# Bringing ScalarE's tables in ahead of the first gates and three attentions, in a fused two-model block kernel

## The chip, the cores and the metric

The kernel runs on one core of one Trainium2 chip, as one launch. Its time is the device time of that launch in microseconds. A core has TensorE (PE in the profile), VectorE (DVE), ScalarE (ACT), GpSimd (POOL) and SyncE (SP), each with an instruction stream of its own; they meet by semaphores.

## What is computed

The input is one sequence of 512 tokens with 1024 features in fp32. A first block is followed by a second block of two layers and a last RMS norm. Cut to what matters:

```python
# first block
h = rms_norm(x, norm_gain); proj = h @ w_in          # q_n, kc, vc, ks, vs, kw, vw, gates, z_n, q_d, k_d, v_d, qi, ki, wi, z_d
g = sigmoid(gate_logits)
o_nsa = g0 * compressed + g1 * selected + g2 * window # 8 heads of 64, times silu(z_n)
o_dsa = attention over the 128 best keys by score = sum_h relu(qi_h . ki) * wi_h   # times silu(z_d)
x = x + concat(o_nsa, o_dsa) @ w_out
# second block, for each of 2 layers
cos, sin = rope_tables(positions)
mod = c @ w_ada + b_ada
h = rms_norm(x) * (1 + sc) + sh; proj = h @ w_in
y_a = rg_lru(conv(x_lru))                             # sigmoid gates, exp(log_a), sqrt
c_q, c_kv = rms_norm(q_down), rms_norm(kv_down)       # latents, 256 and 128 wide
y_b = causal softmax attention of 8 heads of 192, from c_q, c_kv and a roped key   # mla
y = sigmoid(gate_a) * y_a + sigmoid(gate_b) * y_b
x = x + g_m * (y @ w_out); x = x + g_f * (silu(gate) * up) @ w_ffn_out
```

## The kernel before, in words

Everything is written by hand: one function per engine (`block.sync`, `block.gpsimd`, `block.scalar`, `block.vector`, `block.tensor`) writes out that engine's stream in order, with waits on semaphores. There is no scheduler; an engine does its instructions strictly in the order written. X is held transposed, 8 tiles of 128 features by 512 tokens.

**Weights.** All weights come as one stream of 512 KB slots into a ring of seven buffers (RAW). ScalarE copies a slot to its rounded high part (WH, `split_through`, L601), GpSimd (or VectorE for some) subtracts to get the low part (WL, L512), and TensorE does each product as three matmuls (L1894, L1895, L1896: high by high, low by high, high by low). A buffer is refilled once its slot has been passed.

**PSUM.** TensorE takes its eight banks in turn (`claim`) and waits there for whoever read the bank's last content.

**ScalarE's order.** In the first block ScalarE evicts the projection groups in the order 0, 1, 4, 2, 3, 5, 6 (`evict_group`). Group 0 has the index queries (MISC, L704), the index weights (L705) and the gate logits; L707 takes the sigmoid of these, the first in the program. L744 follows with a logarithm for the recurrence's parameters, for which VectorE waits (L1309) before it ropes the index queries. Between groups ScalarE takes the relus of the index scores (`relus(1)`, `relus(2)`, `relus(3)`), which VectorE sums to scores (`index_scores`, L1404, L1409) and reduces by rounds of the eight largest (`topk_round`). Group 2 is the query projection. The cosine and sine of the second block's positions (cs2, tile `cs`) are one activation, L789, that stands behind all evictions of the first block and ahead of its attention; VectorE has the angles ready by L1363 and reads the result only in the second block (`rope2_tables`).

**The three attentions.** The first block's has 96 units of one head pair and one tile of 128 queries; each layer of the second block has one with 32 units. In unit u TensorE makes the scores, VectorE the negated maximum (nmax, L1508 or L1739), ScalarE the exponential (L825 or L959), and TensorE transposes unit u-3 (L2190 or L2320) and, after an eviction, multiplies by the values. In the second block VectorE also scales the exponentials (L1746, L1748) before they are transposed.

**Before a layer's attention.** After the last gate eviction (`"gb"`, tile SG, L609) TensorE transposes the latents and the roped key, 16 transposes (L1992 on KVR). ScalarE evicts them as the high parts CQH and CKH (L920) and as KPE (L924, L925), VectorE makes the low parts (CQL, CKL, L1720), and TensorE's first query product (L1894 on CQH) waits for the two CQL. The value and query products, their evictions and VectorE's roping follow, and then the attention.

**Tables.** A function that the active table lacks needs an ACT_TABLE_LOAD, which is put in directly before the activation; where the activation has more than one wait, the load stands behind all but the last of them. Copy, Identity, Square and Relu have none ahead of them in this program, but for the very first activation (L657).

Of the kernel before, what the change touches and what calls it, by code (L numbers as in the profile page):

```python
# [34 lines left out]
ACT = mybir.ActivationFunctionType  # L35
F32 = mybir.dt.float32
# [5 lines left out]
P = 128  # L42
# [169 lines left out]
def head_square(g, tt):  # L212

    return NT * list(HEAD_GROUPS).index(g) + tt
# [20 lines left out]
def program(nc, a, known):  # L235

    note = {}
    with ExitStack() as ctx:
# [3 lines left out]
        def at(name, shape, dt, off):  # L242
            return nc.alloc_sbuf_tensor_at(name, shape, dt, offset=base + int(off))
# [11 lines left out]
        def small(name, shape, dt, size=4):  # L255
            off = cur[0]
            cur[0] += (int(np.prod(shape[1:])) * size + 31) // 32 * 32
            return at(name, shape, dt, off)
# [5 lines left out]
        vec1 = small("vec1", [P, 3 * KD], F32)  # L264
# [5 lines left out]
        cs2 = small("cs2", [P, 2, NT, HALF], F32)  # L270
# [11 lines left out]
        W0 = (cur[0] + 63) // 64 * 64 + 128  # L282

        def w(name, shape, dt, kb):

            return at(name, shape, dt, W0 + kb * KB)
# [82 lines left out]
        SHA = w("SHA", [P, S], F32, 64)  # L369
        SPREAD = w("SPREAD", [P, S], F32, 66)  # L370

        bank = [ctx.enter_context(nc.psum_tensor(f"bank{i}", [P, S], F32)) for i in range(8)]
        landed = [ctx.enter_context(nc.semaphore(f"slot_landed{i}")) for i in range(RAW_RING)]
        sem = {name: ctx.enter_context(nc.semaphore(name)) for name in SEMAPHORES}
        step = sem["step"]
        count = dict.fromkeys(SEMAPHORES, 0)

        def mark(name, *key, by=1):

            count[name] += by  # L380
            note[(name,) + key] = count[name]
            return by

        def value(*key):

            if known and key not in known:
                raise KeyError(key)
            return known.get(key, 1)
# [6 lines left out]
        def ring(key):  # L395
            return SLOT[key] % RAW_RING

        def loads(key):

            return 16 * (SLOT[key] // RAW_RING + 1)  # L400

        def last_use(key):

            name, v = known.get(("used",) + key, ("full", 1))
            return sem[name], v

        def raw(key):
            return RAW[SLOT[key] % RAW_RING]

        def hi(key):  # L410
            return WH[WSLOT[key] % SPLIT_RING]
# [4 lines left out]
        def bank_of(*key):  # L416

            return bank[known.get(("bank",) + key, 0)]
# [12 lines left out]
        def first_square(k):  # L431

            return (RELU[:, 0, :], RELU[:, 1, :], TMP[:, 0, :], TMP[:, 1, :])[k % 4]
# [156 lines left out]
        def _(act):  # L590
            split_next = [0]

            def split_through(key, ahead=SPLIT_RING - 1):

                last = min(WSLOT[key] + ahead, len(WEIGHTS) - 1)
                while split_next[0] <= last:
                    k = WEIGHTS[split_next[0]]
                    act.wait_ge(landed[ring(k)], loads(k))
                    if split_next[0] >= SPLIT_RING:
                        act.wait_ge(*last_use(WEIGHTS[split_next[0] - SPLIT_RING]))  # L600
                    nc.scalar.activation(hi(k)[:], raw(k)[:], ACT.Copy).then_inc(sem["w_hi"], mark("w_hi", *k))  # L601
                    split_next[0] += 1

            def evict(dst, *key, func=ACT.Copy, **kw):

                act.wait_ge(sem["full"], value("full", *key))
                b = bank_of(*key)
                n = int(np.prod(dst.shape[1:]))
                return nc.scalar.activation(dst, b[0:dst.shape[0], 0:n], func, **kw).then_inc(  # L609
                    sem["read_act"], mark("read_act", *key))  # L610

            def square(tag, k, sq):
                if tag == "n1":
                    if k >= 4:
                        act.wait_ge(sem["n1_added"], value("n1_added", tag, max(1, k - 4)))
                    dst = first_square(k)
                else:
                    if k >= 2:
                        act.wait_ge(sem["sq_added"], value("sq_added", tag, max(1, k - 2)))
                    dst = sq[:, k % 2, :]  # L620
                nc.scalar.activation(dst, X[:, k, :], ACT.Square, scale=float(D) ** -0.5).then_inc(
                    sem["square"], mark("square", tag, k))
# [59 lines left out]
            for k in range(KD):  # L682
# [7 lines left out]
            nc.scalar.activation(lt[:, 1], lt[:, 0], ACT.Exp, scale=-1.0).then_inc(  # L690
                sem["lru_par"], mark("lru_par", 1))
            split_through(("p1", 1, 3), 0)

            def evict_group(g):

                split_through(("p1", g, 3), 0 if g in (2, 3, 6) else SPLIT_RING - 1)
                if g == 0:
                    act.wait_ge(step, value("rstd", "n1"))
                for tt in range(NT):
                    act.wait_ge(sem["full"], value("full", "p1", g, tt))  # L700
                    b = bank_of("p1", g, tt)
                    rstd = stat[:, 1, tt:tt + 1]
                    if g == 0:
                        nc.scalar.activation(MISC[:, tt, :], b[:, 0:384], ACT.Identity, scale=rstd)  # L704
                        nc.scalar.activation(gate[:, tt, 24:28], b[:, 408:412], ACT.Identity,  # L705
                                             scale=stat[:, 2, tt:tt + 1])
                        nc.scalar.activation(gate[:, tt, 0:24], b[:, 384:408], ACT.Sigmoid, scale=rstd).then_inc(  # L707
                            sem["read_act"], mark("read_act", "p1", g, tt))
                    elif g < 5:
                        if g in HEAD_GROUPS:  # L710
                            i = head_square(g, tt)
                            if i >= 4:
                                act.wait_ge(sem["head_sq_read"], value("head_sq_read", i - 4))
                            n = HEAD_GROUPS[g]
                            nc.scalar.activation(HSQ[:, i % 4, 0:n], b[:, 0:n], ACT.Square, scale=rstd).then_inc(
                                sem["head_sq"], mark("head_sq", i))
                        evict(G[g][:, tt, :], "p1", g, tt, func=ACT.Identity, scale=rstd)
                    else:
                        act.wait_ge(sem["iscore"], value("iscore", 3, 3))
                        evict(Z[:, tt, (g - 5) * 512:(g - 4) * 512], "p1", g, tt, func=ACT.Silu, scale=rstd)  # L720

            def relus(qt):
                n = (qt + 1) * P
                for h in range(1, 4):
                    if qt > 1:
                        act.wait_ge(sem["iscore"], value("iscore", qt - 1, h))
                    evict(RELU[:, h - 1, 0:n], "idx", qt, h, func=ACT.Relu)

            def shift_in(kv):


                act.wait_ge(sem["full"], value("full", "tc", kv))
                b = bank_of("tc", kv)
                act.wait_ge(sem["pool_set"], value("pool_set", 1))
                if kv:
                    act.wait_ge(sem["ca"], value("ca", 0, 1))
                for g in range(2):
                    nc.scalar.activation(KC2[0:DH, g, 0:S], b[g * DH:(g + 1) * DH, :], ACT.Copy)
                    last = nc.scalar.activation(KC2[DH:P, g, 0:S - 1], b[g * DH:(g + 1) * DH, 1:S], ACT.Copy)
                last.then_inc(sem["read_act"], mark("read_act", "tc", kv))  # L740
# [8 lines left out]
            relus(1)  # L749
            shift_in(0)  # L750
            evict_group(2)
            relus(2)
            relus(3)
            split_through(("p1", 3, 0))
# [30 lines left out]
                sem["read_act"], mark("read_act", "tkc"))  # L785


            act.wait_ge(step, value("angles"))
            nc.scalar.activation(cs2[:], cs2[:], ACT.Sin).then_inc(sem["cos_sin"], mark("cos_sin"))  # L789


            def scale_ada(i):
# [57 lines left out]
            for layer in range(LAYERS):  # L850
                L = layer

                def vec(col):
                    return par[:, L, col:col + 1]
# [57 lines left out]
                for n in range(KD):  # L912
                    split_through(("gb", L, n))
                    act.wait_ge(sem["ya_gated"], value("ya_gated", L, n))
                    evict(SG[:, n, :], "gb", L, n, func=ACT.Sigmoid)
                for i in range(3):
                    act.wait_ge(sem["full"], value("full", "tc2", L, i))
                    b = bank_of("tc2", L, i)
                    dst = CQH[:, i, :] if i < 2 else CKH[:]
                    nc.scalar.activation(dst, b[:], ACT.Identity, scale=vec(PQG + i)).then_inc(  # L920
                        sem["c_hi"], mark("c_hi", L, i))
# [1589 lines left out]
```

## Time and profile before

| | |
|---|---|
| median of 3 runs | 1813.1 us (1811.85, 1813.1, 1813.21) |
| the profiled execution | 1810.82 us, of which the span from first to last instruction is 1809.0 |
| PE busy | 1744.4 us (96%) |
| DVE busy | 993.7 us (55%) |
| ACT busy | 731.2 us (40%) |
| POOL busy | 693.9 us (38%) |
| mean granted TensorE clock | 0.992 of full |
| ACT_TABLE_LOAD | 27, 1283 ns each |

Times in the trace are microseconds from the first instruction. A row of a timeline is: start, duration, engine, line, operation, output<-inputs, shape, count, and in brackets the idle time of that engine before the row and what ended it. Rows that follow each other and are alike are merged. Activations overlap their neighbours by about 0.1 us. The end of a matmul in the trace is modelled. The granted clock is a share of 2.4 GHz: 1.00 is 2.4 GHz and 0.50 is 1.2 GHz.

### The profile page before, as it was taken

To read this page: it belongs to the slowest core of one execution; us is meant where nothing else is said; L and a number is where in the kernel's file an instruction comes from. 1 tells how busy PE (TensorE), PEld (TensorE's weight loads), DVE (VectorE), ACT (ScalarE), POOL (GpSimd) and SP (SyncE) were. 2 spreads that over 40 slices of the span, in tenths; PEclk is the share of its full clock that TensorE was granted. 3 is DMA by queue.
4 is the path that set the end of the run, shared out by engine and by line. 5 is a ranking of instruction groups with operands and counts; after the bars stand their busy time and mean duration, and the time that the engine had idled before them with its cause. 6 is when DMAs were issued, how large, how long until landed. Compare 5 with 4: busy or idle time off the path is not lost. (4 is left out here: it accounts for less than half of the span.)

```text
span 1809.0 us, 23187 instructions
## 1 busy us (share of the span) xinstructions
PE 1744.4 (96%) x8313; PEld 1415.0 (78%) x8313; DVE 993.7 (55%) x1653; ACT 731.2 (40%) x1258; POOL 693.9 (38%) x305
## 2 busy tenths in 40 slices
PE   7999998989999999999999999999999999999997
PEld 7777777767888766788888888878766888888886
DVE  5999776484679577633333336989665631111112
ACT  6434665523475554322222223456454342222221
POOL 3424111246430333555545557430211644444442
PEclk9999999999999999999999999999999999999998
DMA  7234010063232224355555542322310322232211
GB/s 251 80 104 140 24 36 24 24 209 120 102 105 93 82 82 136 133 198 186 194 188 199 187 140 97 113 82 94 105 36 27 102 93 93 86 112 93 93 59 47
DMA packets 56632, 197.65 MB, mean 109 GB/s; under 512 B 6993, under 2 KB 8017, under 8 KB 56530
## 3 DMA queue, kind: packets, MB, share of 16 engines
q1 hardware_dynamic: 55666, 194.15, 31.5%
q10 hardware_dynamic: 864, 2.11, 0.3%
q8 instruction: 67, 1.10, 0.3%
q14 instruction: 35, 0.29, 0.0%
HBM read 194.14 MB, written 2.10 MB: 108 GB/s over the span
## 5 line engine op out<-in xcount | busy, mean ns | idle before, releaser
L512 POOL TENSOR_TENSOR WL<-RAW,WH 128x1024 fp32r<-128x1024 f32 x234 | 593.7, 2543 | 876.5 <-ACT WH L601 542.1
L1894 PE MATMUL bank<-HH,WH 128*128 128x512 f32 x1120 | 437.3, 390 | 6.8 <-POOLq L517 5.9
L1895 PE MATMUL bank<-HL,WH 128*128 128x512 f32 x1120 | 436.0, 389 | 0.0
L1896 PE MATMUL bank<-HH,WL 128*128 128x512 f32 x1120 | 435.9, 389 | 0.0
L601 ACT ACTIVATE WH<-RAW 128x1024 fp32r<-128x1024 f32 x259 | 270.5, 1051 | 244.6 <-PE bank L1896 220.0
L1894 PEld LDWEIGHTS bank<-HH,WH 128*128 128x128 f32 x1120 | 210.4, 188 | 52.2 <-issue 8.8
L1896 PEld LDWEIGHTS bank<-HH,WL 128*128 128x128 f32 x1120 | 210.4, 188 | 43.9
L1895 PEld LDWEIGHTS bank<-HL,WH 128*128 128x128 f32 x1120 | 210.4, 188 | 43.3
L1814 DVE TENSOR_TENSOR HF<-SILU,bank 128x512 f32<-128x512 f32 x43 | 29.6, 688 | 301.6 <-PE bank L1896 300.6
L1894 PE MATMUL bank<-HDH,WH 128*128 128x512 f32 x352 | 137.1, 389 | 0.0
L1896 PE MATMUL bank<-HDH,WL 128*128 128x512 f32 x352 | 136.9, 389 | 0.0
L1895 PE MATMUL bank<-HDL,WH 128*128 128x512 f32 x352 | 136.9, 389 | 0.0
L1894 PE MATMUL bank<-WH,HH 128*128 128x512 f32 (+2 forms) x288 | 111.9, 389 | 13.7 <-DVE WL L1259 8.4
L1825 DVE SCALAR_TENSOR_TENSOR X<-bank,mod,X 128x512 f32<-128x512 f32 x32 | 24.0, 751 | 174.0 <-PE bank L1896 174.0
L1896 PE MATMUL bank<-WH,HL 128*128 128x512 f32 (+2 forms) x288 | 110.3, 383 | 0.0
L1895 PE MATMUL bank<-WL,HH 128*128 128x512 f32 (+2 forms) x288 | 110.2, 383 | 0.0
L1042 DVE SCALAR_TENSOR_TENSOR ACC<-RAW,vec,ACC 128x1024 f32<-128x1024 f32 x70 | 106.7, 1524 | 4.0
L1002 ACT ACTIVATE HDH<-HF 128x512 fp32r<-128x512 f32 x44 | 27.8, 632 | 191.2 <-DVE HF L1814 190.4
L526 POOL TENSOR_TENSOR ACC<-ACC,RAW 128x1024 f32<-128x1024 f32 x14 | 33.5, 2393 | 139.4 <-ACT RAW L805 139.1
L609 ACT ACTIVATE SILU<-bank 128x512 f32<-128x512 f32 x43 | 25.7, 597 | 129.9 <-PE bank L1896 129.8
L1508 DVE TENSOR_REDUCE nmax<-bank 128x1 f32<-128x128 f32 (+3 forms) x96 | 46.0, 489 | 57.3 <-PE bank L2183 36.9
L1895 PEld LDWEIGHTS bank<-HDL,WH 128*128 128x128 f32 x352 | 66.1, 188 | 13.7
(370 smaller groups left out, 2903.8 us busy)
## 6 DMA issues: line engine op xcount, KB each, us to landing
RAW<-in_stream SPq DMA_DIRECT2D x363, 512.0 KB, 3.3
out_t<-YA SPq DMA_DIRECT2D x8, 256.0 KB, 2.2
X<-in_xt ACTq DMA_DIRECT2D x3, 512.0 KB, 10.9
RAW<-in_stream SPq DMA_DIRECT2D x2, 256.0 KB, 3.8
X<-in_xt ACTq DMA_DIRECT2D x2, 256.0 KB, 6.0
ACC<-in_pos SPq DMA_DIRECT2D x1, 256.0 KB
gains<-in_gains SPq DMA_DIRECT2D x1, 224.0 KB
CS<-in_cs SPq DMA_DIRECT2D x1, 128.0 KB
```

The costliest lines, as they stand in the source:

```text
L512: nc.gpsimd.tensor_tensor(lo(k)[:], raw(k)[:], hi(k)[:].bitcast(F32), ALU.subtract).then_inc(sem["passed"], mark("passed", *k))
L526: nc.gpsimd.tensor_tensor(acc, acc, raw(k)[:], ALU.add).then_inc(sem["ada_sum"], mark("ada_sum", i))
L601: nc.scalar.activation(hi(k)[:], raw(k)[:], ACT.Copy).then_inc(sem["w_hi"], mark("w_hi", *k))
L609: return nc.scalar.activation(dst, b[0:dst.shape[0], 0:n], func, **kw).then_inc(sem["read_act"], mark("read_act", *key))
L1002: nc.scalar.activation(HDH[:, f % FH, :], HF[:, f % 2, :], ACT.Copy).then_inc(sem["hid_hi"], mark("hid_hi", L, f))
L1042: ins = V.scalar_tensor_tensor(out=acc, in0=raw(k)[:], scalar=c, in1=acc, op0=ALU.mult, op1=ALU.add)
L1508: V.tensor_reduce(nmax[:, u % 8:u % 8 + 1], b[:, 0:n], AX_X, ALU.max, negate=True).then_inc(sem["nmax"], mark("nmax", 1, u))
L1814: V.tensor_tensor(HF[:, f % 2, :], SILU[:, f % 2, :], b[:], ALU.mult).then_inc(sem["hid"], mark("hid", L, f))
L1825: ins = V.scalar_tensor_tensor(out=X[:, n, :], in0=b[:], scalar=mod[:, L, 5 * KD + n:5 * KD + n + 1], in1=X[:, n, :], op0=ALU.mult, op1=AL ...
L1894: nc.tensor.matmul(out, A[0], B[0], start=first, stop=False)
L1895: nc.tensor.matmul(out, A[0], B[1], start=False, stop=False)
L1896: return nc.tensor.matmul(out, A[1], B[0], start=False, stop=last)
```

## The change

A tile SCRAP of one column is added, and a helper `table_of(func)` that runs an activation of one column of `vec1` into it. It is called with Sigmoid before group 0 is evicted, with Exp before the first block's attention, and with Exp in each layer of the second block between the last gate eviction and the eviction of the latents. The sine moves from behind all evictions of the first block to behind group 2.

```diff
+        SCRAP = at("SCRAP", [P, 1], F32, W0 - 64)
...
+            def table_of(func):
+
+                nc.scalar.activation(SCRAP[:], vec1[:, 0:1], func)
+
...
             split_through(("p1", 1, 3), 0)
+            table_of(ACT.Sigmoid)
...
             evict_group(2)
+            act.wait_ge(step, value("angles"))
+            nc.scalar.activation(cs2[:], cs2[:], ACT.Sin).then_inc(sem["cos_sin"], mark("cos_sin"))
             relus(2)
             relus(3)
             split_through(("p1", 3, 0))
...
-            act.wait_ge(step, value("angles"))
-            nc.scalar.activation(cs2[:], cs2[:], ACT.Sin).then_inc(sem["cos_sin"], mark("cos_sin"))
+            table_of(ACT.Exp)
...
                     evict(SG[:, n, :], "gb", L, n, func=ACT.Sigmoid)
+                table_of(ACT.Exp)
                 for i in range(3):
                     act.wait_ge(sem["full"], value("full", "tc2", L, i))
```

The loads are not in the source but in the built program, which has 27 before and 28 after. Line numbers of the changed kernel are higher: by 2 up to L609, by more behind it. On ScalarE, around the latents of the first of the two layers (SG is the last gate, CQH and CKH the latents, P the first exponential), the program before has:

```order
L609 ACTIVATE SG<-bank 128x512
L920 ACTIVATE CQH<-bank,par 128x512 x2
L920 ACTIVATE CKH<-bank,par 128x512
L924 ACTIVATE KPE<-bank 64x512
L925 ACTIVATE KPE<-bank 64x512
L601 ACTIVATE WH_62<-RAW_57 128x1024
L609 ACTIVATE QRR<-bank 128x512 x4
L601 ACTIVATE WH_59<-RAW_58 128x1024
L609 ACTIVATE V_143<-bank 128x512 x8
L609 ACTIVATE QN<-bank 128x512 x2
L609 ACTIVATE QRT<-bank 128x512 x4
L959 ACT_TABLE_LOAD
```

The changed program has, at the same place on the same engine:

```order
L611 ACTIVATE SG<-bank 128x512
L616 ACT_TABLE_LOAD
L616 ACTIVATE SCRAP<-vec_71 128x1
L929 ACTIVATE CQH<-bank,par 128x512 x2
L929 ACTIVATE CKH<-bank,par 128x512
L933 ACTIVATE KPE<-bank 64x512
```

The load has moved from behind QRT, where it stood directly ahead of the first exponential, to ahead of CQH, and the one-column activation has come with it. The second layer has the same.

Around the index relus of the first block, on ScalarE (G is the query projection's last eviction, HID the first silu), the program before has:

```order
L609 ACTIVATE G_90<-bank,stat 128x512
L609 ACTIVATE RELU<-bank 128x384 x3
L609 ACTIVATE RELU<-bank 128x512 x3
L601 ACTIVATE WH_59<-RAW_58 128x1024
L601 ACTIVATE WH_60<-RAW_52 128x1024
L601 ACTIVATE WH_61<-RAW_53 128x1024
L601 ACTIVATE WH_62<-RAW_54 128x1024
L609 ACT_TABLE_LOAD
L609 ACTIVATE HID<-bank 64x256
```

and the changed program:

```order
L611 ACTIVATE G_90<-bank,stat 128x512
L760 ACT_TABLE_LOAD
L760 ACTIVATE cs_77<-cs_77 128x256
L611 ACTIVATE RELU<-bank 128x384 x3
L611 ACTIVATE RELU<-bank 128x512 x3
L603 ACTIVATE WH_59<-RAW_58 128x1024
L603 ACTIVATE WH_60<-RAW_52 128x1024
L603 ACTIVATE WH_61<-RAW_53 128x1024
L603 ACTIVATE WH_62<-RAW_54 128x1024
L611 ACT_TABLE_LOAD
L611 ACTIVATE HID<-bank 64x256
```

The sine used the table of the silu before and had no load of its own; at its new place it has one, and the silu's load stays.

## Rows read from the trace of the kernel before

**Rows 1.** The page's busy time by engine: us, share of the span, instructions.
```profile
PE 1744.4 (96%) x8313; PEld 1415.0 (78%) x8313; DVE 993.7 (55%) x1653; ACT 731.2 (40%) x1258; POOL 693.9 (38%) x305
```
**Rows 2.** Groups by line and shape, ScalarE: xcount | busy us, mean ns | idle before.
```profile
L609 ACT ACT_TABLE_LOAD x12 | 15.4, 1283 | 0.2
...
L784 ACT ACTIVATE KCT<-bank 64x32 f32<-64x32 f32 x1 | 0.2, 188 | 0.0
```
**Rows 3.** Timeline of ScalarE at the first gates: start, us, engine, operation [idle before <-releaser].
```profile
33.67 0.58 ACT L704 ACTIVATE MISC<-bank,stat 128x384 f32<-128x384 f32 x1 [3.53 <-DVE stat L1284]
...
34.41 1.28 ACT L707 ACT_TABLE_LOAD   x1
35.70 0.28 ACT L707 ACTIVATE gate<-bank,stat 128x24 f32<-128x24 f32 x1
```
**Rows 4.** Timelines of TensorE and VectorE at the first gates.
```profile
36.03 0.50 PE L1894 MATMUL bank<-WH,HH 128*128 128x512 f32 x1 [1.17 <-ACT gate L707]
...
40.00 0.17 DVE L1309 TENSOR_TENSOR lt<-lt 128x16 f32<-128x16 f32 x1 [4.18 <-ACT lt L744]
```
**Rows 5.** Stretch 40 to 107 us: length, then busy PE, PEld, DVE, ACT, POOL.
```profile
40.00:107.00 67.00, 64.18 (x294) 50.88 (x293) 63.62 (x145) 26.55 (x41) 23.87 (x10) 1.00 0.19 63
```
**Rows 6.** Timelines of ScalarE, VectorE and TensorE behind the query projection.
```profile
105.09 1.26 ACT L609 ACTIVATE RELU<-bank 128x384 f32<-128x384 f32 x3
...
106.61 0.62 DVE L1404 TENSOR_SCALAR SCORE<-bank,gate 128x384 f32<-128x384 f32 x1
107.27 1.93 DVE L1409 SCALAR_TENSOR_TENSOR SCORE<-RELU,gate,SCORE 128x384 f32<-128x384 f32 x3
...
107.49 0.83 PE L2080 MATMUL bank<-RAW,CA 128*64 128x256 f32 x3 [0.39 <-DVE SCORE L1404]
```
**Rows 7.** Timelines of ScalarE, VectorE and TensorE at the first attention's start.
```profile
198.95 0.42 ACT L789 ACTIVATE cs<-cs 128x256 f32<-128x256 f32 x1
199.78 1.28 ACT L825 ACT_TABLE_LOAD   x1 [0.41 <-PE bank L2183]
...
202.46 0.89 DVE L1508 TENSOR_REDUCE nmax<-bank 128x1 f32<-128x256 f32 x2
...
201.58 0.33 PE L2190 MATMUL bank<-ident,PR 128*128 128x128 f32 x1 [0.47 <-ACT PR L825]
...
205.57 0.66 PE L2202 MATMUL bank<-G,PT 128*128 128x64 f32 x4 [0.24 <-ACT PT L609]
```
**Rows 8.** Timelines of ScalarE, VectorE and TensorE at the latents, and the second layer's wait.
```profile
597.03 0.60 ACT L609 ACTIVATE SG<-bank 128x512 f32<-128x512 f32 x1 [3.90 <-PE bank L1896]
597.52 1.26 ACT L920 ACTIVATE CQH<-bank,par 128x512 fp32r<-128x512 f32 x2
...
598.32 1.41 DVE L1720 SCALAR_TENSOR_TENSOR CQL<-bank,par,CQH 128x512 fp32r<-128x512 f32 x2 [10.49 <-PE bank L1992]
...
599.83 0.47 PE L1894 MATMUL bank<-WH,CQH 128*128 128x512 f32 x1 [1.15 <-issue]
...
1292.02 0.47 PE L1894 MATMUL bank<-WH,CQH 128*128 128x512 f32 x1 [1.15 <-issue]
```
**Rows 9.** Timelines of ScalarE, VectorE and TensorE at the first layer's attention.
```profile
618.53 1.28 ACT L959 ACT_TABLE_LOAD   x1 [0.92 <-PE bank L2313]
...
620.51 0.29 DVE L1748 TENSOR_SCALAR P<-P,coef 128x128 f32<-128x128 f32 x1
...
622.49 0.28 PE L2320 MATMUL bank<-ident,P 128*128 128x128 f32 x1
```
**Rows 10.** TensorE behind two idle times, and stretches with the granted clock behind POOL.
```profile
407.09 0.47 PE L1894 MATMUL bank<-HH,WH 128*128 128x512 f32 x1 [2.52 <-POOLq L517]
...
1187.71 0.71 PE L1894 MATMUL bank<-XCH,WH 128*128 128x512 f32 x1 [2.79 <-DVE XCL L1648]
...
1187.80:1191.20 3.40, 3.40 (x8) 2.64 (x9) 3.24 (x2) 3.40 (x7) 3.25 (x2) 0.50 0.00 0
1191.20:1195.00 3.80, 3.80 (x18) 3.13 (x17) 0.00 (x0) 3.77 (x6) 2.11 (x1) 0.99 0.56 164
```

## The prediction

> **What bounds the kernel now.** The busy times come first: PE has work in 96% of the span, and no other engine has more than 55% [rows 1]. A ScalarE instruction therefore costs or gives time only where TensorE stands still for it. So I looked up every table load in the groups by line [rows 2] and read, around each that moves, the timelines of the three engines: does TensorE wait there, for whom, and until when? That gives five places. The reader should see that what counts at each is the idle time in brackets on TensorE's row, not the 1.28 us of the load.
>
> The price of the moved pieces: a load takes 1.283 us [rows 2], and its neighbours join it without a gap, since the gate's load starts at 34.41 and the gate itself at 35.70 [rows 3]. A load breaks the overlap of about 0.1 us that neighbouring activations have: the gate at 597.03 runs 0.60, to 597.63, and the next starts at 597.52 [rows 8]. The one-column activation isn't in the trace; the nearest row is the 32-column one of 0.188 us [rows 2]. Bounds are zero and those 0.19 us; I take 0.19. With both put in between two busy activations, the second starts later by 0.01 + 1.28 + 0.01 + 0.19, plus one overlap of 0.1 that is lost (the one behind SCRAP remains): about **1.5 us**.
>
> The Trainium skill, page "ScalarE: Activation LUTs", section "What ACT_TABLE_LOAD costs", counts a drain of some 1.38 us on top of the 1.283, 2.66 in all. The rows leave no room for it, as 34.41 + 1.28 is 35.69 and the gate starts at 35.70. By the page's price two of the delays below would be 1.4 us longer each and the sum 2.8 us higher.
>
> **First gates: a gain of 1.2 us.** ScalarE is idle for 3.53 us before the first eviction [rows 3], so load and SCRAP (1.5 us) fit there and cost nothing. Without the load the first gate ends 1.28 us earlier. TensorE waited 1.17 us for exactly that [rows 4]; its previous matmul keeps it busy until then, so it gets 1.17 and not 1.28. Does it last? The next in line is VectorE, which waits at 40.00 for the logarithm behind these gates [rows 4] and is then busy 63.62 of 67 us up to the index scores [rows 5], for which TensorE waits at 107.49 [rows 6]. The logarithm moves by the same 1.28, so both chains move. Nothing that doesn't move ends a wait later, as DMA arrivals follow the slots passed. Bounds: 0 (some other chain holds) and 1.28. I take 1.2.
>
> **The sine: a loss of 0.1 us.** VectorE makes the angles (up to L1363) before it ropes the keys, well ahead of the query projection, so the wait is free. But the sine brings a load of its own, 1.28 us, beside its own 0.42 [rows 7]. Three relus that started at 105.09 start about 1.7 us later, at 106.8. VectorE is busy with its rounds until 106.61, scores without them until 107.23, and takes the first relu at 107.27 [rows 6]. One relu takes a third of 1.26 with overlap, so the first is there at 107.3 and the rest keep ahead of VectorE's 0.65 each. VectorE is late by about 0.1. TensorE's wait at 107.49 is for L1404, which needs no relu, so even that 0.1 may vanish. The cover is VectorE's rounds; were they 1.5 us shorter, the whole 1.7 would show. Taking the sine away from its old place gives nothing: ScalarE waits there for the scores anyway [rows 7]. Bounds: 0 and 1.7; I take 0.1.
>
> **First attention: 0.** The load starts at 199.78 behind the first scores [rows 7]; now it starts where the sine stood, at 198.95 [rows 7], with SCRAP behind it, and the first exponential starts at about 200.3 in place of 201.07. TensorE's wait of 0.47 at 201.58 goes. What is late next is VectorE: a top-k round of its own holds the maximum of unit 3 until 202.46, and with it the fourth exponential and all of ScalarE's list behind it, so TensorE meets its wait at 205.57 at the same time, as 0.7 in place of 0.24 [rows 7]. The gain is between 0 and 0.47; I take 0.
>
> **The latents, twice: a loss of 1.5 us each.** ScalarE ends the last gate and begins CQH at once (597.52, no idle in brackets); VectorE's two CQL follow it from 598.32 for 1.41 us, to 599.73; TensorE starts its query product at 599.83, having been idle 1.15 us [rows 8]. That is a chain without slack, ScalarE to VectorE to TensorE. The gate can't go earlier: it waited 3.90 us for TensorE. So the 1.5 us of load and SCRAP go straight into TensorE's idle time, which becomes 2.7 us. The second layer shows the same 1.15 [rows 8]. Queued behind are also CKH, KPE and a weight split, all due later than CQL. Bounds: 1.3 (SCRAP free, overlap kept) and 1.6; I take 1.5, so 3.0 in all.
>
> **Their attentions: 0.** The load there starts at 618.53 and delays the first exponential by 1.0 us. But TensorE transposes it only in unit 3, behind four units of scores without a break, at 622.49, while VectorE has it scaled by 620.80 [rows 9]: 1.7 us of slack. What the early table frees was hidden. Bounds: 0 and 1.0 each; I take 0.
>
> **The clock.** Two idle times grow from 1.15 to 2.7. Behind an idle time of 2.79 the granted clock was 0.50, 1.2 GHz, for 3.4 us, and TensorE began 8 matmuls in it where it began 18 in the next 3.80, or 16 in 3.4 [rows 10]: 8 times 0.21 is 1.7 us lost. Behind an idle time of 2.52 there was no such loss: the next matmul took 0.47 there against 0.71 [rows 10]. The new 2.7 lies between, with 16 short transposes ahead of it. I give each place an even chance in each execution, at 1.6 us (bounds 0 and 1.7).
>
> **Sum.** -1.2 + 0.1 + 0 + 3.0 + 0 = +1.9 us with the clock left out, and +3.5 with one fall of it, the likeliest of the three. The profiled execution took 1810.82 and the three runs 1811.85, 1813.1 and 1813.21: the median of all four is 1812.5, between the profiled one and the stated median. I set the sum on that: 1812.5 + 3.5 = **1816.0 us**, 2.9 above the stated median. On the profiled execution alone it would be 1814.3.
>
> **Rivals.**
> - *The clock falls at both places in most executions.* The added idle time decides it; for it speaks that the transposes ahead are short, against it that 2.52 did nothing. It decides if the two come out at 2.79 or above, where the clock did fall. +1.9 + 3.2 = +5.1: 1817.6. Chance 0.17. This one ends on the slower side.
> - *It falls at neither.* +1.9: 1814.4. Chance 0.18.
> - *The early table does what it says.* If TensorE's waits for evictions within the attentions hang on ScalarE's head start, each exponential that comes 1.0 earlier pays, and 0.47 more in the first: up to 2.5 us. If besides ScalarE waits at CQH for the transposes, the 3.0 goes too. Against both stand rows without an idle bracket at CQH and with 1.7 us of slack [rows 8, 9]. -1.1 to -3.6: 1808.9 to 1811.4. Chance 0.10.
> - *The sine's 1.7 us reaches TensorE* by the relus, if VectorE comes to them earlier than before. +3.5 + 1.6 = +5.1: 1817.6. Chance 0.03.
> - *A load holds ScalarE for longer than its row*, by as much again as the row has. Two more of 1.28 at the latents make +6.1: 1818.6. The 0.01 us between load and gate speak against it [rows 3]. Chance 0.02. (This is the drain of the page above.)
>
> The forecast itself has 0.50.
>
> **How the numbers follow.** A measurement can tell about 0.2%, 3.6 us, from no change; slower starts at 1816.7. The forecast at 1816.0 with about 1.5 us of scatter gives 0.33 within and 0.17 above; the rivals give 0.20 above (both clocks 0.15, sine and longer load 0.05), 0.25 within, and 0.05 below. Faster 0.05, same 0.58, slower 0.37. The range leaves out half of the third rival and the tail above both clock falls: 1812.3 to 1818.6.
>
> **What would show it.** Right: no wait for the gate at 36; the idle time at L1894 on CQH 2.6 to 2.7 in both layers, with SCRAP ahead of CQH; half clock behind one of them or both; TensorE's wait in place of 205.57 grown to 0.7; the first transposes of the layers' attentions as tight as before; 28 loads of 1.28. Wrong: an idle time of 1.15 left at the latents, a first transpose that comes earlier against its scores, or a wait for relus ahead of L1404 or L2080.

## The result, and the profile after

The change makes the kernel slower by 6.1 us: the median of 13 runs is 1819.47 us (1816.52 to 1823.52) against 1813.39 us (1810.13 to 1816.45) for 13 runs of the kernel before on the same chip. The ratio is 1.0036, with a 95% interval of 1.0028 to 1.0044. That is above the 0.2% that can be told from no change. The forecast was 1816.0 and the range ended at 1818.6, so the result lies 0.9 us outside it.

One caution ahead of the rows. The profiled execution of the changed kernel took 1823.52 us and is the slowest of its 13, and its span is 12.6 us longer than that of before. The traces are read here for what happens at each place; the size of the whole is read from the medians.

The page of the changed kernel, busy time by engine, answers to [rows 1]:

```profile
PE 1756.4 (96%) x8313; PEld 1421.9 (78%) x8313; DVE 991.7 (54%) x1653; ACT 732.9 (40%) x1263; POOL 693.8 (38%) x305
```

ScalarE has five instructions more: four one-column activations and one table load. TensorE has not one instruction more and yet is busy for 12.0 us longer. The same matmuls took longer, so the granted clock is where to look. The groups by line and shape (count | busy us, mean ns | idle before) give the price of the pieces:

```profile
L616 ACT ACT_TABLE_LOAD x4 | 5.1, 1283 | 0.1
...
L616 ACT ACTIVATE SCRAP<-vec 128x1 f32<-128x1 f32 x4 | 0.8, 203 | 0.0
```

A load is what it was in [rows 2], 1283 ns. A one-column activation takes 203 ns, where I took 0.19 us.

**First gates.** The timelines of ScalarE and TensorE, to be read beside [rows 3, 4] (start, us, engine, operation, [idle before <-releaser]):

```profile
30.24 1.28 ACT L616 ACT_TABLE_LOAD   x1
...
34.17 0.58 ACT L711 ACTIVATE MISC<-bank,stat 128x384 f32<-128x384 f32 x1 [2.43 <-DVE stat L1293]
34.80 0.28 ACT L714 ACTIVATE gate<-bank,stat 128x24 f32<-128x24 f32 x1
...
35.13 0.50 PE L1903 MATMUL bank<-WH,HH 128*128 128x512 f32 x1
```

The load has moved into ScalarE's idle time, and 2.43 us of that are left. TensorE has no bracket any more where it had 1.17 us of waiting for the gate. Against the trace of before it comes 1.0 us earlier by this.

**The sine.** The three timelines behind the query projection, beside [rows 6]:

```profile
105.23 0.68 ACT L611 ACTIVATE G<-bank,stat 128x512 f32<-128x512 f32 x1
105.93 1.28 ACT L760 ACT_TABLE_LOAD   x1
107.22 0.42 ACT L760 ACTIVATE cs<-cs 128x256 f32<-128x256 f32 x1
107.54 3.13 ACT L611 ACTIVATE RELU<-bank 128x384 f32<-128x384 f32 x6
...
108.12 1.93 DVE L1418 SCALAR_TENSOR_TENSOR SCORE<-RELU,gate,SCORE 128x384 f32<-128x384 f32 x3 [0.18 <-ACT RELU L611]
...
108.19 0.62 PE L2089 MATMUL bank<-RAW,CA 128*64 128x256 f32 x2 [0.38 <-DVE SCORE L1413]
```

The relus come 1.7 us later behind G (2.31 us behind its start, where it was 0.57), VectorE waits 0.18 us for the first of them, and TensorE waits 0.38 us where it waited 0.39.

**First attention's start,** beside [rows 7]:

```profile
201.19 1.28 ACT L616 ACT_TABLE_LOAD   x1
...
203.19 0.28 PE L2199 MATMUL bank<-ident,PR 128*128 128x128 f32 x1
...
205.94 0.43 PE L2211 MATMUL bank<-G,PT 128*128 128x64 f32 x2 [0.43 <-ACT PT L611]
...
207.81 0.66 PE L2211 MATMUL bank<-G,PT 128*128 128x64 f32 x4 [0.24 <-ACT PT L611]
```

TensorE's 0.47 us ahead of the first transposes is gone. The wait that takes its place, 0.43 us, stands in front of the product that ran at 203.80 before, without a wait. The wait of 0.24 us behind it, at 205.57 before [rows 7] and at 207.81 now, is as long as it was. For that time TensorE was 0.70 us ahead, and behind the new wait it has given all of it back. What holds it is VectorE's maximum for unit 3: ScalarE now waits 1.12 us for it, where it waited 0.41, and evicts the PT of that product only behind it:

```profile
205.16 0.47 ACT L833 ACTIVATE PR<-bank,nmax 128x256 f32<-128x256 f32 x1 [1.12 <-DVE nmax L1517]
```

From there on the two traces run at the distance that they had ahead of the attention, to within 0.01 us.

**The latents,** beside [rows 8]:

```profile
598.78 0.60 ACT L611 ACTIVATE SG<-bank 128x512 f32<-128x512 f32 x1 [3.90 <-PE bank L1905]
599.39 1.28 ACT L616 ACT_TABLE_LOAD   x1
600.69 0.20 ACT L616 ACTIVATE SCRAP<-vec 128x1 f32<-128x1 f32 x1
600.80 1.25 ACT L929 ACTIVATE CQH<-bank,par 128x512 fp32r<-128x512 f32 x2
...
601.58 1.41 DVE L1729 SCALAR_TENSOR_TENSOR CQL<-bank,par,CQH 128x512 fp32r<-128x512 f32 x2 [12.00 <-ACT CQH L929]
...
603.09 0.76 PE L1903 MATMUL bank<-WH,CQH 128*128 128x512 f32 x1 [2.66 <-issue]
...
1301.23 0.47 PE L1903 MATMUL bank<-WH,CQH 128*128 128x512 f32 x1 [2.66 <-issue]
```

From the start of SG to the start of CQH it was 0.49 us before and is 2.02 us now. The whole 1.5 us arrives at TensorE, whose idle time grows from 1.15 to 2.66 us, in both layers. And then the clock. Stretches of time behind the two waits (length, then busy PE, PEld, DVE, ACT and POOL with counts of instructions, the granted clock, the DMA share, GB/s):

```profile
602.40:609.30 6.90, 6.21 (x15) 4.89 (x16) 4.28 (x11) 3.52 (x6) 2.37 (x1) 0.51 0.09 33
...
1302.20:1305.60 3.40, 3.40 (x9) 2.65 (x8) 1.67 (x2) 1.31 (x2) 2.37 (x1) 0.50 0.00 0
1305.60:1309.00 3.40, 3.40 (x16) 2.75 (x15) 3.30 (x8) 1.58 (x3) 0.00 (x0) 1.00 0.45 154
```

TensorE ran at 1.2 GHz for 6.9 us behind the first wait and for 3.4 us behind the second. The second is the plain case: 9 matmuls in 3.4 us, and 16 in the next 3.4. In the kernel before, neither place has any half clock.

**The layers' attentions.** TensorE has its first scores at 623.84 and its first transpose at 628.62, 4.78 us apart:

```profile
623.84 0.46 PE L2318 MATMUL bank<-KN,QN 128*128 128x128 f32 x2 [0.89 <-issue]
...
628.62 0.28 PE L2329 MATMUL bank<-ident,P 128*128 128x128 f32 x1
```

Before, they were at 617.71 and 622.49 [rows 9], also 4.78 us apart. The early table gave nothing here.

### The profile page after: what moved, and what is told of

Read it like the earlier page. It is cut to its first block and busy times, and to the rows that moved or that the text cites. A ratio compares the mean times of both kernels' runs of the same rounds, so it can differ in the third digit from the quotient of the medians.

```text
span 1821.6 us, 23192 instructions
## 1 busy us (share of the span) xinstructions
PE 1756.4 (96%) x8313; PEld 1421.9 (78%) x8313; DVE 991.7 (54%) x1653; ACT 732.9 (40%) x1263; POOL 693.8 (38%) x305
## 5 line engine op out<-in xcount | busy, mean ns | idle before, releaser
L1905 PEld LDWEIGHTS bank<-HDH,WL 128*128 128x128 f32 x352 | 66.1, 188 | 13.7
```

The costliest lines, as they stand in the source:

```text
L1905: return nc.tensor.matmul(out, A[1], B[0], start=False, stop=last)
```

## Experiments

Three theories about the 6.1 us had to be told apart: that the two tables at the latents and the clock behind them are all of it; that the sine takes part; and that part of it is only in the profiled execution. All of the runs stand below. The first four share 27 runs of the kernel before with a median of 1813.03 us, the next four share 25 with 1812.66 us.

**Without the latents' tables.** The change with one line taken out:

```diff
                     evict(SG[:, n, :], "gb", L, n, func=ACT.Sigmoid)
-                table_of(ACT.Exp)
                 for i in range(3):
```

> The change without the two one-column Exp activations ahead of the latents; the load is again directly ahead of each layer's first exponential. Theory A (all of the loss sits at the latents: 3.0 us of delay and the rest TensorE's clock falling behind the longer idle time): 1 us faster than before, ratio 0.9994 (0.9985 to 1.0003), idle time ahead of the first product on CQH 1.15 again. Theory B (the moves in the first block, gates, sine and first exponentials, shift things so that the clock falls there, and the latents cost 3.0 alone): 3 us slower than before, ratio 1.0017.

Measured: 1811.21 us, ratio 0.9990 (0.9981 to 1.0000). The change turns from 6.1 us slower to 1.8 us faster by the medians, at the edge of what the interval lets one call a gain. TensorE waits at the latents for what it waited before:

```profile
599.30 0.47 PE L1902 MATMUL bank<-WH,CQH 128*128 128x512 f32 x1 [1.15 <-issue]
```

All of the loss hangs on this one line. What is left of the change is a gain of the size that the gates should give.

**The latents' tables alone.** The kernel before with the helper and the same single call added:

```diff
                     evict(SG[:, n, :], "gb", L, n, func=ACT.Sigmoid)
+                table_of(ACT.Exp)
                 for i in range(3):
```

> The kernel before with only the one-column Exp ahead of the latents in each layer. Theory A: 7 us slower than before, ratio 1.004, idle time 2.66 at CQH in both layers and half clock behind one or both. Theory B: 3.0 us slower, ratio 1.0017, with no half clock there beyond chance.

Measured: 1819.5 us in 5 runs, ratio 1.0038 (1.0024 to 1.0052), so +6.5 us. Taking the line out gave 7.9 us (6.1 + 1.8) and putting it in gives 6.5 us, and with intervals of 1.5 to 2.5 us either way the two agree. The idle time is 2.66 us in both layers, and in the profiled execution the clock fell behind the second only:

```profile
1299.41 0.47 PE L1901 MATMUL bank<-WH,CQH 128*128 128x512 f32 x1 [2.66 <-issue]
```

```profile
604.00:607.40 3.40, 3.27 (x15) 2.74 (x16) 2.15 (x7) 2.60 (x5) 1.44 (x1) 1.00 0.00 0
1299.80:1303.20 3.40, 3.40 (x10) 2.66 (x9) 1.18 (x6) 1.87 (x3) 1.96 (x1) 0.50 0.00 0
```

**The change with something to do in the wait.** Ten matmuls on constant tiles are put behind the transposes of the latents, into a bank that nobody reads:

```diff
                 turn(("tc2", L, 3), [KVR[:, tt, 384:448] for tt in range(NT)], rows=DH)
+                warm("tc2", L, 10)
```

> The change, and TensorE fills its idle time at the latents with ten matmuls of 512 columns on constants, into a bank that nobody reads, behind the 16 transposes (2.3 us). ScalarE's delay stays, only the idle time goes. Theory A with the clock as the larger part: 1.9 us slower than before, ratio 1.001 (1.0003 to 1.0018), 4 us faster than the change, no half clock between the latents and the attention in either layer. Theory C (the clock does nothing there, the loss is ScalarE's lateness in what follows): as slow as the change, ratio 1.0034.

Measured: 1814.84 us, ratio 1.0014 (1.0005 to 1.0023), so +1.8 us. The table still holds ScalarE, but the added matmuls fill most of the wait, and the clock stays at full behind both:

```profile
598.44 2.10 PE L2056 MATMUL bank<-keep,identb 128*128 128x512 bf16 x9
...
601.05 0.47 PE L1903 MATMUL bank<-WH,CQH 128*128 128x512 f32 x1 [0.50 <-issue]
```

```profile
601.00:604.40 3.40, 3.35 (x15) 2.79 (x16) 2.14 (x6) 2.58 (x5) 1.52 (x1) 1.00 0.00 0
1296.40:1299.80 3.40, 3.40 (x15) 2.81 (x16) 2.13 (x6) 2.59 (x5) 1.56 (x1) 1.00 0.00 0
```

The filler doesn't bring the query product forward, since its operands are as late as in the change. What it takes away is the clock's part: 1819.47 - 1814.84 = 4.6 us by the medians, or 6.1 - 1.8 = 4.3 us against the two sets of runs of before. What it leaves, +1.8, is near the +1.9 that the prediction summed with the clock left out. The agreement is partly luck: the profile of this run has falls of the clock in other places that the kernel before lacks (at 699.9 and 751.1 us), and lacks the one that the kernel before has behind its wait for XCL.

**The sine alone.** The kernel before with only the sine at its new place:

```diff
             evict_group(2)
+            act.wait_ge(step, value("angles"))
+            nc.scalar.activation(cs2[:], cs2[:], ACT.Sin).then_inc(sem["cos_sin"], mark("cos_sin"))
```

> The kernel before with only the sine moved behind the query projection, where it has a load of its own. Theory A: 0 to 0.2 us slower, ratio 1.0000, relus(2) 1.7 us later against the projection's last eviction and VectorE's scores 0.1 later, TensorE's idle time ahead of the first product on CA 0.4 as before. Theory B with the sine as its cause: 1.5 to 3 us slower, ratio 1.001 or more.

Measured: 1812.13 us, ratio 1.0000 (0.9991 to 1.0009). The load comes at 105.88, as in the change, and VectorE waits 0.19 us:

```profile
108.07 1.27 DVE L1408 SCALAR_TENSOR_TENSOR SCORE<-RELU,gate,SCORE 128x384 f32<-128x384 f32 x2 [0.19 <-ACT RELU L609]
```

No part of the loss shows with the sine alone.

**The gate's table alone.** The kernel before with only the first call:

```diff
             split_through(("p1", 1, 3), 0)
+            table_of(ACT.Sigmoid)
```

> The kernel before with only the one-column Sigmoid ahead of group 0. The 1.17 us that TensorE waits for the first gate go, and the chain through VectorE moves with it: 1.2 us faster, ratio 0.9993 (0.9985 to 1.0001); 1 us or more of it is still there when the first attention starts, unless the clock falls before that. If the gain were lost on the way: ratio 1.0000.

Measured: 1811.25 us, ratio 0.9996 (0.9987 to 1.0004), 1.4 us below by the medians. The interval alone would not show a gain. The trace does: TensorE's wait of 1.17 us [rows 4] is down to 0.15 us. TensorE had been 0.2 us ahead of the trace of before already, is 1.2 us ahead behind the gates and 1.1 us at 272 us, so that some 0.9 us of the gain is still there.

```profile
34.83 0.50 PE L1901 MATMUL bank<-WH,HH 128*128 128x512 f32 x1 [0.15 <-ACT gate L714]
```

**The table behind the latents.** The change with the call moved ahead of the two QN evictions. ScalarE's stream is slack there, and the table is still ready before the first exponential:

```diff
-                table_of(ACT.Exp)
                 for i in range(3):
...
+                table_of(ACT.Exp)
                 for h in range(2):
                     evict(QN[:, h, :], "qn", L, h, scale=float(QK) ** -0.5)
```

> The change with the one-column Exp of each layer moved from ahead of the latents to ahead of the first two evictions of QN, where ScalarE was idle for 1.4 us. The table is in before the first exponential, without lateness at the latents. If the head start of 1 us at the attention's start is worth something: 2 us faster than without it, ratio to before 0.998. If the layers' first exponentials were hidden all along (my reading): as the change without any latent tables, 1 to 2 us faster than before, ratio 0.9990, and the first transposes of the attention just as tight behind the scores.

Measured: 1812.97 us, ratio 1.0001 (0.9992 to 1.0010). The gain of 1 to 2 us that I had expected from the rest of the change doesn't show here, though the gate's wait is gone in this trace too. The wait at the latents is 1.15 us again. The first exponential finds its table and then waits 1.20 us for VectorE's maximum, and the first transpose keeps its 4.78 us behind the scores:

```profile
619.44 0.37 ACT L968 ACTIVATE P<-bank,nmax 128x128 f32<-128x128 f32 x1 [1.20 <-DVE nmax L1748]
...
618.34 0.46 PE L2318 MATMUL bank<-KN,QN 128*128 128x128 f32 x2 [0.89 <-issue]
...
623.12 0.28 PE L2329 MATMUL bank<-ident,P 128*128 128x128 f32 x1
```

So even a table that costs TensorE nothing at the latents gives nothing at the attention's first transpose.

**Three tables at each latents.** Two more loads and two more one-column activations, so that the price per load and what comes behind it show in larger numbers:

```diff
                 table_of(ACT.Exp)
+                nc.scalar.activation(SCRAP2[:, 0:1], vec1[:, 0:1], ACT.Sigmoid)
+                nc.scalar.activation(SCRAP2[:, 1:2], vec1[:, 0:1], ACT.Exp)
```

> The change with two more loads and two more one-column activations in each layer ahead of the latents (Sigmoid and Exp again, into columns of their own), so three of each. Idle time at CQH 2.66 + 2.8 = 5.5 us in both layers. If the lateness passes through one for one and the clock has fallen about as often as it can already: 5.6 to 7 us slower than the change, 12 to 13 us slower than before, ratio 1.007. If something downstream takes lateness up: under 4 us slower than the change, ratio under 1.0055. If the half clock grows with the idle time: ratio 1.0085 or more.

Measured: 1825.14 us in 4 runs, ratio 1.0072 (1.0057 to 1.0086), +12.5 us.

```profile
603.85 0.76 PE L1906 MATMUL bank<-WH,CQH 128*128 128x512 f32 x1 [5.67 <-issue]
```

The idle time is 5.67 us in both layers (I had expected 5.5): 4.52 more than 1.15 for three, or 1.51 for each, the same as for one. The granted clock is at half for 6.8 us in each layer, but 3.0 us of that stretch in the first layer and 2.6 us in the second lie within the idle time, so only 1.8 and 2.0 us are lost behind it:

```profile
600.90:607.70 6.80, 3.85 (x9) 3.11 (x10) 2.83 (x8) 5.18 (x9) 2.03 (x1) 0.50 0.00 0
```

The delay is proportional to the loads, and the clock's part isn't: it is paid about once for each place.

**The change again, four times.** One profile can't tell how often the clock falls. The changed kernel itself was run four more times, each with a profile.

> The change once more, for a profile of another execution: how often the clock falls behind the longer idle time at the latents. By my prediction (an even chance at each place, 1.6 us) half of the places show it. If each of the four new profiles shows it at both places or nearly, or for twice as long as 3.4 us, the missing 2.5 us of my sum are the clock's.

> As the look before it: two more places at the latents, where the idle time itself is 2.66 us in both layers each time, and where by my prediction one of two shows half clock.

> As the two looks before it: two more places at the latents, where the idle time itself is 2.66 us, and by my prediction one of the two shows half clock.

> As the three looks before it: two more places at the latents, where the idle time itself is 2.66 us, and by my prediction one of the two shows half clock.

Measured: 1816.71, 1817.67, 1817.73 and 1818.92 us, against 1811.12 us for the kernel before. The stretches behind the waits, of the first run:

```profile
600.20:603.60 3.40, 3.27 (x8) 2.62 (x9) 1.23 (x6) 2.11 (x4) 1.44 (x1) 0.50 0.00 0
1296.50:1299.90 3.40, 3.40 (x9) 2.63 (x10) 0.98 (x5) 2.14 (x3) 1.69 (x1) 0.50 0.00 0
```

The other three show the same. How far TensorE falls behind the kernel before during these stretches, in us:

| profile | idle, each layer | lost to the clock, first layer | second layer |
|---|---|---|---|
| the change | 2.66 | 2.87 (twice 3.4 us at half) | 1.65 |
| again, 1 | 2.66 | 1.53 | 1.60 |
| again, 2 | 2.66 | 1.40 | 1.60 |
| again, 3 | 2.66 | 1.56 | 1.59 |
| again, 4 | 2.66 | 1.47 | 1.62 |
| latents' tables alone | 2.66 | 0 | 1.59 |

In the change the clock fell in 10 of 10 places, and in 11 of 12 with the run of the tables alone. The ten falls cost 1.69 us each in the mean, so 3.4 us for an execution.

The same traces show a second part of the loss, further on. In all five profiles of the change the clock falls once more in the norm behind the first layer's attention, where TensorE has 16 matmuls of one column and a wait of 0.79 us; in the first run again:

```profile
750.40:753.80 3.40, 3.40 (x11) 1.75 (x11) 1.67 (x10) 0.00 (x0) 0.00 (x0) 0.50 0.05 20
```

Between 640 and 1180 us the five lose 3.5, 0.8, 1.9, 0.9 and 1.9 us in this way, in the table's order (the first has one more fall, at 704.9 us). The other three runs that have the tables at the latents lose 1.6 (the tables alone), 3.6 (with the filler) and 0.8 us (three tables). The kernel before and the five runs without tables at the latents have no fall in that stretch. What brings these falls about wasn't tested. The filler at the latents doesn't prevent them.

**Fillers where the kernel before waits.** If a short wait costs a clock fall on top, then waits that the kernel before already has should be worth filling. This one takes the change without the latents' tables and adds matmuls on constants in two places. They were meant to fill the first block's last wait, for MIX, and the second layer's wait for XCL [rows 10]:

```diff
+            warm("mix", 0, 13)
             pe.wait_ge(sem["gmix"], value("gmix", NT - 1))
...
+                        if (L, q, i) == (1, 0, 2):
+                            warm("lg", 1, 11)
                         pe.wait_ge(sem["xc_lo"], value("xc_lo", L, n))
```

> The change without the latent tables, and with filler matmuls of 512 columns on constants in two of TensorE's longest idle times: thirteen ahead of the transposes of MIX (3.3 us idle) and eleven in the second layer where it waits for XCL (2.8 us idle). No work that counts is earlier; only the clock may be held. If the half clock behind idle time costs what its rows say: 2 to 5 us faster than the same without fillers, ratio to before 0.997, no half clock behind these two places. If it costs nothing on the path, or the fillers make the transposes late: ratio 0.999 or more.

Measured: 1807.3 us in 7 runs, ratio 0.9974 (0.9964 to 0.9985), 5.4 us faster than the kernel before. The same kernel without the fillers was 1.8 us faster than its own set of runs of before; the fillers are thus worth some 3.5 us (3.9 by the two medians). It beats both kernels. The stretch 362 to 372 us in the kernel before:

```profile
362.00:372.00 10.00, 6.73 (x35) 6.59 (x36) 3.63 (x6) 3.35 (x6) 2.34 (x1) 0.66 0.00 0
```

and with the fillers, where the second line is the place of the second layer's wait for XCL, which had 0.50 behind it in [rows 10]:

```profile
362.00:372.00 10.00, 9.53 (x63) 7.32 (x63) 5.25 (x9) 4.03 (x8) 2.35 (x1) 1.00 0.00 1
1183.00:1187.00 4.00, 4.00 (x19) 3.30 (x19) 3.25 (x2) 3.82 (x7) 3.86 (x2) 1.00 0.06 10
```

The 32 transposes of MIX take 3.71 us now, against 6.54 us at the lower clock:

```profile
366.06 3.71 PE L2000 MATMUL bank<-ident,MIX 128*128 128x128 f32 x32 [0.47 <-POOL MIX L575]
```

They start no later than before, so this filler does what it was meant to. The second doesn't. The condition `(1, 0, 2)` puts it into the first quarter of the recurrence's gates, where TensorE didn't wait, and the wait of 2.79 us is in the next quarter:

```profile
1162.93 2.55 PE L2055 MATMUL bank<-keep,identb 128*128 128x512 bf16 x11
```

It delays TensorE by 2.4 us there. Some 20 us later the whole wait for XCL is gone, and TensorE comes out 2.3 us further ahead of the kernel before than it went in. One part of that is that TensorE arrives later. Another is that VectorE, which makes XCL, arrives earlier: its eight multiplications by the latents' norms (L1617, L1618), in which two instructions took 2.4 us or more in the kernel before and one does here, take 4.2 us in place of 6.2. So this place doesn't show what filling a wait is worth, and no run has one filler without the other.

## Why the prediction was wrong by 3.5 us

**The step that failed is the clock's chance.** The text reads: "I give each place an even chance in each execution, at 1.6 us." So the sum holds one fall of 1.6 us. The price was right: nine of the ten falls in the change cost 1.40 to 1.65 us. The chance was not. The clock fell at both places in all five profiles of the change, and 3.2 to 3.4 us stand where the sum has 1.6. The likeliest case was therefore the first rival, "the clock falls at both places in most executions", +5.1 us, to which I gave 0.17.

The even chance came from two rows of one execution, 2.52 us of waiting without a fall and 2.79 us with one [rows 10], with 2.66 between them. Neither row is what that wait always does. In the traces of the later runs the wait of the first row is 2.46 to 2.52 us long each time, and the clock fell behind it in 8 of the 14 profiles. In the profiled execution of the change it did:

```profile
407.66 0.57 PE L1903 MATMUL bank<-HH,WH 128*128 128x512 f32 x1 [2.46 <-POOLq L519]
```

```profile
407.90:411.30 3.40, 3.40 (x9) 2.63 (x9) 1.30 (x2) 1.19 (x2) 3.40 (x2) 0.50 0.76 265
```

Behind the wait of the second row, 2.69 to 2.80 us long, it fell in 9 of 13 (the run with the fillers has no such wait). At these two waits somewhat over one half is what the runs show. At the latents it is 11 of 12, and the cause of that difference stays open. The 16 short transposes ahead of the latents' wait, where long matmuls stand ahead of the other two, are the candidate that the prediction names and gives no weight; no run changed them alone.

**A second term stood at nothing.** The prediction prices the clock only directly behind the two waits. All five profiles of the change have more falls further on, between 640 and 1180 us, which cost 0.8 to 3.5 us and which no profile without tables at the latents has.

**The gates: right by the traces, a little high.** Forecast -1.2. The step in the change's trace is -1.0 us, and it is -1.0 with the gate's table alone, of which 0.9 us are still there at 272 us. By the medians it is -1.4 alone and -1.8 for the change without the latents' tables, but +0.3 for the run with the table ahead of QN, which has the same gates. Of the three only the -1.8 reaches the edge of its noise.

**The sine: right.** Forecast +0.1 with VectorE late by 0.1. VectorE waits 0.18 us, TensorE gets nothing of it, and the kernel with the sine alone is at 1.0000.

**The first attention: right, 0, with the wait in another place.** TensorE gained 0.70 us up to the transposes behind 203.58 and gave it back at the next product. The holder was the one that I named, VectorE's maximum of unit 3. The forecast that the wait at 205.57 would grow to 0.7 was wrong. That one stayed at 0.24 us, and a new one of 0.43 us stands one product ahead of it.

**The latents: right.** Forecast 1.5 us each; measured 1.51 us each in all profiles, and 1.51 for each of three loads. The terms as I wrote them out add up to 1.59; SCRAP's own overlap with CQH, 0.1 us, has to come off to give 1.5. The three-table run also ends the dispute over a longer hold. With a drain of the size that the Trainium skill gives (page "ScalarE: Activation LUTs", section "What ACT_TABLE_LOAD costs"), each load would have delayed CQH by 1.4 us more. The rows have 0.02 us between the load's end (599.39 + 1.28 = 600.67) and the next activation at 600.69.

**The layers' attentions: right, 0.** The 4.78 us between scores and transpose didn't move, neither with the early table nor with the one behind the latents.

**The sum as it should have read:** -1.2 + 0.1 + 3.0 + 3.2 = +5.1 us. On the 1813.4 us of the kernel before in the 13 paired runs that is 1818.5, against 1819.47 measured. My base of 1812.5 was 0.9 low; it had moved off the stated median towards a single profiled execution. So of the 3.5 us that were missing, 1.6 are the second fall at the latents, 0.9 the base, and about 1 us is left. The falls between 640 and 1180 us are large enough for it. They aren't a clean sum, because in three of the five profiles of the change the fall behind the wait for XCL is missing in return, at 1.6 us. How falls in one place and in another hang together stays open.

## What to carry to other kernels

A table load is worth moving only to a place where its engine is idle, and only if somebody waits where it stood. The gate's table met both conditions and gained 1.0 us in the traces. The latents' table met neither, since the chain from ScalarE over VectorE to TensorE had no slack there and four units of scores covered its old place.

A delay that lengthens a wait of TensorE should be priced with the clock behind it. Here 1.5 us of delay at each place cost 3.1. One row of one execution doesn't say whether a wait has a fall behind it: the same wait of 2.5 us had one in 8 of 14 profiles. Several profiles of the kernel before are the thing to take first.

Look the other way too: existing waits can cost more than their idle time. Two short runs of matmuls on constants won more (some 3.5 us) than the whole change was worth at its best (1.8 us), though only one of the two stood at a wait.

## What the runs showed of the hardware that I hadn't expected

The clock can fall behind far shorter waits than 2.5 us. In the profiled execution of the change it was at half behind an idle time of 1.88 us and again at the end of one of 1.45 us, both next to short transposes:

```profile
55.01 1.62 PE L2001 MATMUL bank<-ident,MISC 128*128 128x128 f32 x12 [1.88 <-DVE MISC L1198]
56.29 0.76 PE L1903 MATMUL bank<-WH,HH 128*128 128x512 f32 x1
...
115.78 0.66 PE L2001 MATMUL bank<-ident,G 128*128 128x128 f32 x4
117.89 0.79 PE L1903 MATMUL bank<-WH,HH 128*128 128x512 f32 x1 [1.45 <-POOL WL L514]
```

The kernel before has the first of these waits too, and its clock held:

```profile
55.91 0.77 PE L1992 MATMUL bank<-ident,MISC 128*128 128x128 f32 x5 [1.89 <-DVE MISC L1189]
```

Each of these two waits is there in all 14 profiles (1.62 to 1.93 and 1.45 to 1.48 us), and each has a fall in 3 of them. So at such places the outcome differs between executions, while at others it doesn't: the clock fell between 364 and 372 us, at a wait of 3.27 us, in every profile of a kernel without the fillers, 13 of them, and at the latents in every one of the change. What makes a place one or the other stays open.

A one-column activation isn't cheap: it takes 203 ns, where the eviction of 32 columns from a bank, with another function, takes 188 ns [rows 2]. In the chain at the latents it added 0.11 us (600.69 to 600.80), and the load 1.4: 1.30 from its start to SCRAP, and 0.12 by which it starts later behind SG than CQH did (0.61 for 0.49).
